# Three reorderings of vector and scalar work in a fused five-layer transformer kernel on one core

## The reference

```python
def _mla_branch(x, w_in, q_norm, w_q_up, kv_norm, w_kv_up, w_out):
    h = x @ w_in
    cq, ckv, k_rope, gate = h[..., :384], h[..., 384:640], h[..., 640:672], h[..., 672:]
    q = (_rmsnorm(cq, q_norm) @ w_q_up).reshape(B, S, 16, 64 + 32)
    kv = (_rmsnorm(ckv, kv_norm) @ w_kv_up).reshape(B, S, 16, 64 + 64)
    # rope on the last 32 of q and on k_rope, which all heads share
    o = _dense_causal(q_full, k_full, v, 96 ** -0.5).reshape(B, S, 1024)
    return (o * silu(gate)) @ w_out
```

## Time and profile before

| | |
|---|---|
| median of 3 runs | 1687.75 us (1687.68 to 1689.03) |
| the profiled execution | 1687.05 us |
| its span | 1684.9 us |
| PE busy | 1650.9 us |
| DVE busy | 787.9 us (47%) |
| ACT busy | 768.2 us (46%) |
| POOL busy | 613.9 us (36%) |

### The profile page before, as it was taken

One profiled execution on the slowest core, in us unless ns is written; L12 is line 12 of the kernel. 1 busy time (PEld: TensorE's weight loads), 2 busy tenths in 40 slices (PEclk: granted clock), 3 DMA queues, 4 the chain that ended last, 5 costly groups with the idle time before them and its releaser, 6 DMA issues.

```text
span 1684.9 us, 24286 instructions
## 1 busy us (share of the span) xinstructions
PE 1650.9 (98%) x9349; PEld 1341.7 (80%) x9349; DVE 787.9 (47%) x2038; ACT 768.2 (46%) x1565; POOL 613.9 (36%) x298
## 2 busy tenths in 40 slices
PE   8999999999999999999999999999999999999998
PEld 7777779777888787778777778777788888888877
DVE  3777636566344434436777636888141111001052
ACT  4566634566243535434566725336753222222252
POOL 4323224332243323234322224692144444444423
PEclk9999999999999999999999999999999999999999
DMA  6322144323542222154323154432153332333422
GB/s 171 69 45 74 49 152 142 78 60 66 154 146 75 77 63 79 45 173 111 65 45 83 40 163 143 130 89 75 40 174 100 100 95 93 100 100 88 125 63 88
DMA packets 216046, 161.17 MB, mean 96 GB/s; under 512 B 53755, under 2 KB 197147, under 8 KB 215932
## 3 DMA queue, kind: packets, MB, share of 16 engines
q1 hardware_dynamic: 205904, 130.21, 27.5%
q10 hardware_dynamic: 9804, 29.38, 5.6%
q0 software_dynamic: 224, 0.03, 0.1%
HBM read 148.32 MB, written 11.14 MB: 95 GB/s over the span
## 4 chain that ended last, share of the span: by engine, by line
PE 83%; DVE 9%; ACT 5%; POOL 2%; issue 1%; DMA 0%; ACTq 0%; DVEq 0%; SPq 0%; POOLq 0%
PE banks L481 23%; PE banks L483 22%; PE banks L482 22%; PE banks L740 5%; PE banks L701 4%; PE banks L755 4%; PE banks L906 1%; PE banks L724 1%; ACT AB L1487 1%; DVE AB L2231 1%; ACT G L1616 1%; ACT w_hi L1357 1%; DVE misc L2626 1%; PE banks L714 1%; POOL w_lo L2821 1%
## 5 line engine op out<-in xcount | busy, mean ns | idle before, releaser
L2821 POOL TENSOR_TENSOR w_lo<-w_raw,w_hi 128x1024 fp32r<-128x1024 f32 (+2 forms) x253 | 573.1, 2275 | 1038.9 <-ACT w_hi L1357 1028.1
L481 PE MATMUL banks<-XTh,w_hi 128*128 128x512 f32 (+5 forms) x1216 | 451.2, 371 | 3.8 <-DVE XTl L2290 1.4
L483 PE MATMUL banks<-XTh,w_lo 128*128 128x512 f32 (+5 forms) x1216 | 444.0, 365 | 0.0
L482 PE MATMUL banks<-XTl,w_hi 128*128 128x512 f32 (+5 forms) x1216 | 443.9, 365 | 0.0
L1357 ACT ACTIVATE w_hi<-w_raw 128x1024 fp32r<-128x1024 f32 (+4 forms) x254 | 250.3, 995 | 154.8 <-PE banks L483 107.4
L481 PEld LDWEIGHTS banks<-XTh,w_hi 128*128 128x128 f32 (+2 forms) x1216 | 227.7, 187 | 47.3 <-issue 6.8
L483 PEld LDWEIGHTS banks<-XTh,w_lo 128*128 128x128 f32 (+2 forms) x1216 | 227.7, 187 | 38.2
L482 PEld LDWEIGHTS banks<-XTl,w_hi 128*128 128x128 f32 (+2 forms) x1216 | 227.8, 187 | 37.0 <-issue 1.2
L481 PE MATMUL banks<-w_hi,OTh 128*128 128x512 f32 (+1 forms) x448 | 173.0, 386 | 1.9 <-DVE QKl L2055 1.8
L483 PE MATMUL banks<-w_hi,OTl 128*128 128x512 f32 (+1 forms) x448 | 167.9, 375 | 0.0
L482 PE MATMUL banks<-w_lo,OTh 128*128 128x512 f32 (+1 forms) x448 | 167.7, 374 | 0.0
(11 more groups left out here) (212 smaller groups left out, 2342.9 us busy)
## 6 DMA issues: line engine op xcount, KB each, us to landing
w_raw<-in_w_gate_up_dram SPq DMA_DIRECT2D x44, 512.0 KB, 3.8
w_raw<-in_fox_w_in_dram SPq DMA_DIRECT2D x30, 512.0 KB, 4.1
w_raw<-in_mla_w_in_dram SPq DMA_DIRECT2D x26, 512.0 KB, 4.7
w_raw<-in_w_in_dram SPq DMA_DIRECT2D x24, 512.0 KB, 3.9
w_raw<-in_w_down_dram SPq DMA_DIRECT2D x22, 512.0 KB, 3.5
w_raw<-in_swa_w_in_dram SPq DMA_DIRECT2D x20, 512.0 KB, 4.1
w_raw<-in_mla_w_out_dram SPq DMA_DIRECT2D x16, 512.0 KB, 3.7
x_spill<-AB ACTq DMA_DIRECT2D x16, 512.0 KB, 2.6
```

Of the source, the lines that this page charges most:

```text
L481: nc.tensor.matmul(o, ah, bh, start=first, stop=False, skip_group_check=True)
L482: nc.tensor.matmul(o, ah, bl, start=False, stop=False, skip_group_check=True)
L483: return nc.tensor.matmul(o, al, bh, start=False, stop=last, skip_group_check=True)
L2821: pool.tensor_tensor(view(w_lo, u, RING), view(w_raw, u, RAW), view(w_hi, u, RING).bitcast(F32), ALU.subtract).then_inc(lo_done, 1)
```

## The change

Five edits in three places:

1. Odd rounds of the latent layers (1 and 3). DVE takes the second key's low part in position 4, behind the rope sum and ahead of the first head's norm. ACT writes the query's high part before the split that it followed, likewise the first key's, and the second key's high part between the third and the fourth exponential of the second head (`fill(i - 1, 7)`). DVE takes the last maxima of pair i + 2 inside `mixed`, behind the output's scaling, and no longer ahead of it (`mixed_first`).
2. Opening of the latent layers. DVE's reciprocal for the key and value latents, the three low latents, the first gate and the two scalings come ahead of the three copies of the rotated key; the second gate and the two last low latents follow.
3. Window layer, round -1. The norm of the second head of pair 0 is cut in two: the sum, the reciprocal and two tiles ahead of the query's low part, two tiles behind it (`norm_split`).

```diff
@@ ACT, exps @@
                     for t in range(T):
+                        if x == 1 and t == T - 1:
+                            fill(i - 1, 7)
                         sc = pr.score(b, x, t)
@@ ACT, fill of the latent layers @@
-                        if pos == 5:
+                        if pos == 5 and i < 0:
                             rope(g)
                             query(i + 3)
-                            if i > 0:
-                                keys(g, 0)
+                        elif pos == 5:
+                            rope(g)
+                            hi(QKh[:, 3 + (i + 3) % 2, :], group()[:, :])
+                            advance()
+                            hi(QKh[:, 2 * g % 3, :], group()[:, :])
+                            advance()
+                        elif pos == 7 and i > 0:
+                            keys(g, 1)
...
                         elif pos == 2:
-                            keys(g, 1)
+                            if i < 0:
+                                keys(g, 1)
                             rotated(g)
@@ DVE, pair_attention @@
-                def norm(i, x):
+                def norm(i, x, t0=0, t1=T):
...
-                    for t in range(T):
+                    for t in range(t0, t1):
...
-                    ins.then_inc(pnorm, 1)
+                    if t1 == T:
+                        ins.then_inc(pnorm, 1)
...
                         src = otmp[:, :]
+                    if i in mixed_first:
+                        maxima(i + 2, 2)
                     fill(i, 3)
...
                     norm(i + 1, 0)
+                    if i == norm_split:
+                        norm(i + 1, 1, 0, 2)
                     fill(i, 1)
-                    if i not in norm_last:
+                    if i == norm_split:
+                        norm(i + 1, 1, 2, T)
+                    elif i not in norm_last:
                         norm(i + 1, 1)
                     fill(i, 2)
-                    maxima(i + 2, 2)
+                    if i not in mixed_first:
+                        maxima(i + 2, 2)
@@ DVE, mla @@
                 lo(QKl[0:ROPE, 7, :], RA[0:ROPE, :], QKh[0:ROPE, 7, :]).then_inc(kr_done, 1)
+                c.g += 1
+                inverse_root(1, c.g)
+                for i in range(3):
+                    low_latent(i)
+                gate(0)
+                gate_at[0] = c.g
+                scaled(1, 3, 5)
                 dve.wait_ge(kr_done, 7 * j + 4)
                 for n in range(1, 4):
                     nc.vector.tensor_copy(...)
-                for i in range(3):
-                    low_latent(i)
-                c.g += 1
-                root_at = c.g
-                gate(0)
-                gate_at[0] = c.g
-                inverse_root(1, root_at)
-                scaled(1, 3, 5)
                 gate(1)
@@ DVE, fill of the latent layers @@
                             rope_sum()
+                            if i > 0:
+                                keys(g, 1)
...
                         elif pos == 2:
                             if i < 0:
                                 keys(g, 0)
-                            keys(g, 1)
+                                keys(g, 1)
                             rope_high(g)
@@ calls @@
-                pair_attention(mla_pairs(), fill, norm_last=(1, 3))
+                pair_attention(mla_pairs(), fill, norm_last=(1, 3), mixed_first=(1, 3))
-            pair_attention(swa_pairs(), fill)
+            pair_attention(swa_pairs(), fill, norm_split=-1)
```

More of the change, by code:

```diff
@@ L2179, in _, with pair_attention @@
             gate_at = {}
-            def pair_attention(pairs, fill, norm_last=()):
+            def pair_attention(pairs, fill, norm_last=(), mixed_first=(), norm_split=None):
                 a0, n_pairs = c.pair, len(pairs)
@@ L2222, in norm @@
                     b, ns = a % 2, slice(4 * x, 4 * x + 4)
[L2223 to L2229, removed]
-                    for t in range(T):
+                    if t0 == 0:
+                        dve.wait_ge(pexp, 2 * a + x + 1)
+                        if pr.sinks is not None:
+                            link(nc.vector.tensor_tensor(rs[:, b, ns], rs[:, b, ns], es[:, b, ns], ALU.add))
+                        if pr.gate is None:
+                            nc.vector.reciprocal(ri[:, b, ns], rs[:, b, ns]).then_inc(pinv, 1)
+                            return
+                        link(nc.vector.reciprocal(ri[:, b, ns], rs[:, b, ns]))
+                    for t in range(t0, t1):
                         ins = nc.vector.tensor_scalar(pr.score(b, x, t), pr.score(b, x, t), ri[:, b, 4 * x + t:4 * x + t + 1],
                                                       None, ALU.mult, ALU.add, accum_out=unused[:, t:t + 1])
-                    ins.then_inc(pnorm, 1)
+                    if t1 == T:
+                        ins.then_inc(pnorm, 1)
                 def mixed(i):
```

## The result

| | median us | runs | ratio to before (95%) |
|---|---|---|---|
| before | 1687.89 | 12 | |
| after | 1692.28 | 12 | 1.0028 (1.0021 to 1.0036) |
| after, a second series | 1692.49 | 9 | 1.0026 (1.0016 to 1.0036) |

The forecast was 1690.2, its range ended at 1691.9. The direction was right and the size was not: +4.4 us instead of +2.4. The profiled execution took 1691.68 us, its span is 1689.6. The ratio isn't that of the two medians but is worked out from the single runs; the two differ by up to 0.0006 here.

The account below looks back on a forecast made before the run. PE, busy 98% of the span, was taken as the bound. Openings +2.8, odd rounds +0.45 and sliding layer -0.87 made +2.4 us, 1689.4 from the profiled 1687.05; with 0.7 to the median, 1690.2 us, range 1684.8 to 1691.9.

Parts of the forecast that it names:

- it fits in the idle stretch with 0.2 us to spare: Sliding layer: the first half norm, 1.07 us, fits DVE's 1.29 us idle stretch before the query's low part; gain 0.87 us.
- the 0.87 wait gone: Sliding layer, sign to look for: PE's 0.87 us wait for pair 0's second norm at 319.49 us disappears.
- from the profiled execution to the median: Last step of the sum: the median of the runs shown, 1687.75, lies 0.7 us above the profiled 1687.05.
- The opening: Both latent layers: POOL's 2.40 us instruction holds DVE's first scaling, so query and first keys start later; +1.4 us each.
- the tie: Latent opening: DVE's product of line 2446, at 67.11, beats POOL's next instruction, at 67.14; +1.4 us, otherwise +2.1.
- Odd rounds: Latent layers: round 3 loses 0.3 and 0.4 us, round 1 gains 0.15 and 0.1; sum +0.45 us.
- The stall at the third transpose: Odd rounds: the next pair's second norm comes 0.96 us later, giving PE a new stall of about 0.35 us.
- The second half of the values: Odd rounds: PE's start, set by the output's scaling, gains 0.53 us in round 1 and nothing in round 3.
- Rival 1: Latent openings: POOL goes ahead of line 2446's product in one or both, +0.7 or +1.4 us, 1690.9 to 1691.6; chance 0.20.
- Rivals 2 and 4: Opening scalings not held by POOL: 1684.7 us, chance 0.13; that plus odd rounds' full gains: 1680.7 us, chance 0.07.
- rival 3: Odd rounds give what they aim at, up to 0.9 us each, -3.6 us in all, 1686.1 us; chance 0.13.
- Rival 2: Latent openings: nothing holds the scalings, so each opening gains 1.3 us, 1684.7 us; chance 0.13.

Follow-up runs that it names:

- window_sum_early: Kernel before with only the sliding layer's norm in halves, both halves' sums in one instruction ahead of the first norm and POOL's instruction; 1687.08 us, ratio 0.9989.
- after_pe_busy: Changed kernel plus unused PE transposes where PE idled: 15 and 8 in both latent openings, 8 near 1034 us; 1690.69 us, ratio 1.0015.
- rounds_alone: Kernel before with only the edits of odd rounds 1 and 3 of the latent layers; 1687.57 us, ratio 0.9994.
- pool_late: Kernel before with the latent opening edit, and ACT's second weight split moved behind the second gate and two high latents; 1693.9 us, ratio 1.0039.
- copies_late: Kernel before with the latent opening edit, but DVE's three key copies moved behind the second keys' low part; 1694.12 us, ratio 1.003.
- before_pe_busy: Kernel before with only 8 unused PE transposes in the idle stretch near 1034 us; 1689.11 us, ratio 0.9999.

## Why the prediction was wrong

- **The step whose mechanism failed: "it fits in the idle stretch with 0.2 us to spare"** (sliding layer, -0.87). It took the half norm's 1.07 us from a place where POOL was idle (behind 317.01 us) and set it down inside POOL's instruction of 314.62, without the rule that the opening's step had used. It measured +0.14. The sign that it gave, "the 0.87 wait gone", came true and misled: the time went to the scores, which started 1.07 us later. window_sum_early shows the rest of that step's reasoning right (-0.94).
  The Trainium skill, page SBUF — State Buffer, section Who interferes with whom, has both halves of it: two inputs in SBUF contend with a GpSimd instruction that reads SBUF; at most one input doesn't, outside the two-port modes, and the tensor_scalar form that also writes its accumulator is not among those that enter them. The runs agree: 1.53 us for the sum beside POOL, and 0.17, 0.35 and 0.48 us for the reciprocal and the tiles beside it, as without it.
- **The term that put the median outside the range: from the profiled execution to the median.** The prediction's sum adds 0.7 us for it (1687.05 to 1687.75) and nothing for the clock; that execution had no stretch at the lower clock within its work. With the edits' 2.24 it makes 1689.3, and the median, 1692.28, is 3.0 above that. Both profiles of the changed kernel have one such stretch, 1.6 us each, and after_pe_busy gets 1.8 us back. This is what carried the median past 1691.9: runs of before without such a stretch lie near 1687.6, the edits' 2.24 make 1689.8 of it, and with PE kept at work the median is 1690.69, inside the range. What the other 0.9 us are is open; late weights near 1025 us are one candidate.
- **The opening: mechanism right, size 1.4 against 1.14.** Scalings, query, first keys and the tie came within 0.1 us of the working, though the tie was called on 0.03 us, which is luck; measured, DVE led by 0.17. The working's own starts give 1.30 and not 1.4 (67.2 + 1.47, against 67.37 for the second keys of before). Measured are 1.24 there and 1.14 from the next matmul on: in before, PE restarted its second keys from a wait.
- **Odd rounds: +0.45 against -0.18.** Right in kind: no wait ahead of the second keys, 0.67 on the output's scaling in round 3 (0.13 in round 1, where 0.5 to 0.8 was named too). The stall at the third transpose shows as no wait in the view, but PE's starts slip 0.20 us a round there, and not 0.35. The second half of the values comes 0.61 us earlier in round 1 and 0.08 in round 3, where the working had 0.53 and 0.
- **Rival 1** (POOL wins the tie) did not come. Rivals 2 and 4 fell with the held scalings, rival 3 with the rounds (-0.15 us in rounds_alone, against -3.6). Rival 2's premise was sound where POOL is away: pool_late.

## What to carry to other kernels

When vector work is moved, lay POOL's instructions over the new place and check every moved instruction with two inputs in SBUF, the smallest too: a four-column sum of 0.15 us took 1.53. An idle stretch is worth what fits beside the other engine; here the reciprocal and the tensor_scalar with an accumulator fitted where the sum didn't. A wait of PE can be followed by a stretch at the lower clock that costs as much again, and an execution without such a stretch is no base for a median that has them.

## What was not expected of the hardware

- A held instruction of four columns ended 0.01 us behind POOL's; those of 512 columns ended about 0.55 behind, as in the earlier trace rows.
- Two instructions issued 0.03 to 0.04 us before POOL's begin (63.52 in before, 62.98 in copies_late) were not held, one issued 0.06 us after it was, and took 2.87 us instead of 0.69.
- Within the work, each stretch at the lower clock began within 3 us of the end of a wait of PE of 0.9 to 2.5 us. The wait near 1034 us had one behind it in 8 of the 14 profiles that left it as it was, the waits of 1.9 us ahead of the query in 2 of 6. They lasted 3.41 us but for one of 6.83 and one of 17.07. Behind 1034 us one of 3.41 cost 1.6 us each time (PE's lag went from 2.69 to 4.32 in the changed kernel), inside the openings 0.4 and 0.7. None of the four profiles with unused transposes in such a wait had a stretch behind it; four profiles are few, and of the medians that of after_pe_busy bears it out and that of before_pe_busy doesn't.
